# A hybrid layer's state-space scan on Trainium2: rotated second products against transfers that swap real and imaginary rows

## The reference

```python
xn = rmsnorm(x, norm_g)
u_a, z_a, q, k, v, z_b, g_a, g_b = split(xn @ w_in)
# S5: 64 groups of 16 channels, 64 complex states each
h[t] = a_bar * h[t-1] + b_bar @ u[t]            # complex
y_a = real(C @ h) + D * u                       # also returned: h at the last position
y_a = gelu(y_a); y_a = y_a * sigmoid(y_a @ glu_w + glu_b) * silu(z_a)
o = stick_breaking_attention(q, k, v) * silu(z_b)
x + (sigmoid(g_a) * (y_a @ w_a) + sigmoid(g_b) * (o @ w_b)) @ w_out, then rmsnorm
```

## Time and profile before

| | |
|---|---|
| median of 3 runs | 3242.06 us (3238.5 to 3243.9) |
| the profiled execution | 3239.77 us, span 3238.0 us |
| TensorE busy | 3127.3 us (97%), 20272 products |
| VectorE, ScalarE, GpSimd busy | 1007.5, 999.5, 756.1 us |
| mean granted TensorE clock | 0.985 of full speed |
| 160 loads of w_in | 512 KB each, 3.9 us to landing |

### The profile page before, as it was taken

The page is one execution under the profiler, slowest core; times in us unless marked ns, Lnnn a source line. Parts: engine busy times, 40 slices in busy tenths (PEclk is TensorE's granted clock), DMA queues, the critical chain, the costliest instruction groups (busy, mean ns, idle before and its releaser), DMA issues.

```text
span 3238.0 us, 50469 instructions
## 1 busy us (share of the span) xinstructions
PE 3127.3 (97%) x20272; PEld 3047.1 (94%) x20272; DVE 1007.5 (31%) x1345; ACT 999.5 (31%) x1258; POOL 756.1 (23%) x2309
## 2 busy tenths in 40 slices
PE   7999999999999999999999999999999999999997
PEld 6998999999899999989999998999899999999997
DVE  5124212312421231242123124212465214332265
ACT  5225214422531442253144225214421101121142
POOL 5620550163055016305501630550013000000000
PEclk9999999999999999999999999999999989999999
DMA  5221122222112222211222221122339545342283
GB/s 170 58 83 59 52 78 71 69 59 83 59 52 78 68 73 59 83 59 52 78 68 73 59 83 59 52 78 69 128 124 293 176 150 177 98 137 71 65 246 106
DMA packets 395785, 304.10 MB, mean 94 GB/s; under 512 B 57314, under 2 KB 364082, under 8 KB 393522
## 3 DMA queue, kind: packets, MB, share of 16 engines
q1 hardware_dynamic: 395570, 301.05, 30.4%
HBM read 227.30 MB, written 65.27 MB: 90 GB/s over the span
## 4 chain that ended last, share of the span: by engine, by line
PE 84%; POOL 5%; ACT 3%; DVE 3%; issue 2%; DMA 1%; SPq 1%; POOLq 0%; DVEq 0%; ACTq 0%
PE acc L1652 71%; PE side L1613 5%; PE side L1821 2%; PE side L1876 1%; PE side L1816 1%; PE acc L1613 1%; ACT L809 1%; POOL work L1164 1%; POOL work L1161 1%; DMA t_oz<-work 1%; POOL work L1158 1%; DMA work<-t_state_seeds 1%; POOL work L1165 1%; POOL work L1160 1%; DVE work L1419 1%
## 5 line engine op out<-in xcount | busy, mean ns | idle before, releaser
L1652 PE MATMUL acc<-x_high,w_high 128*128 128x344 f32 (+2 forms) x5440 | 1230.1, 329 | 15.3 <-issue 3.8
L1652 PE MATMUL acc<-x_low,w_high 128*128 128x344 f32 (+2 forms) x5440 | 1186.3, 321 | 0.0
L1652 PE MATMUL acc<-x_high,w_low 128*128 128x344 f32 (+2 forms) x5440 | 1180.7, 320 | 0.0
L1652 PEld LDWEIGHTS acc<-x_high,w_high 128*128 128x128 f32 x5440 | 913.5, 190 | 41.1 <-issue 23.3
L1652 PEld LDWEIGHTS acc<-x_low,w_high 128*128 128x128 f32 x5440 | 927.2, 190 | 0.0
L1652 PEld LDWEIGHTS acc<-x_high,w_low 128*128 128x128 f32 x5440 | 917.0, 189 | 0.0
L1277 DVE TENSOR_TENSOR w_low<-w_raw,w_high 128x1024 fp32r<-128x1024 f32 x233 | 298.9, 1283 | 1038.2 <-ACT w_high L815 1037.9
L815 ACT CAST w_high<-w_raw 128x1024 fp32r<-128x1024 f32 x232 | 242.9, 1047 | 992.4 <-PE acc L1652 931.3
L1148 POOL COPY work<-s_tables 128x28 f32 x16 | 3.3, 207 | 1370.1 <-DMA work<-t_state_seeds 1370.1
L1613 PE MATMUL side<-work 128*128 128x128 f32 (+6 forms) x832 | 152.7, 308 | 9.7 <-DVE work L1405 9.7
L1613 PEld LDWEIGHTS side<-work 128*128 128x128 f32 (+3 forms) x832 | 100.2, 159 | 43.0 <-issue 25.6
(11 more groups left out here) (296 smaller groups left out, 2524.9 us busy)
## 6 DMA issues: line engine op xcount, KB each, us to landing
w_raw<-in_w_in SPq DMA_DIRECT2D x160, 512.0 KB, 3.9
w_raw<-in_w_out SPq DMA_DIRECT2D x48, 512.0 KB, 4.0
work<-t_sig_ga SPq DMA_DIRECT2D x24, 516.0 KB, 4.5
out<-work SPq DMA_DIRECT2D x18, 512.0 KB
t_sig_gb<-stage SPq DMA_DIRECT2D x16, 516.0 KB, 4.2
t_qk<-stage SPq DMA_DIRECT2D x16, 516.0 KB, 5.2
work<-t_qk SPq DMA_DIRECT2D x16, 516.0 KB, 4.1
t_sig_ga<-stage SPq DMA_DIRECT2D x16, 516.0 KB, 4.1
```

Of the source, the lines that this page charges most:

```text
L1652: ins = mm(acc[s][:, a, 0:n], w[b][:, kk, :], x[:, kx, c0:c0 + n], start=start, stop=stop)
```

## The change

M2 is still computed but no longer transposed, and the products with B2T are gone. VectorE copies the first products from `side` to T2, and two transfers put T2's real rows into the imaginary rows of `swapped_p` and the reverse; this takes the place of Q. After the scan the same is done with T2 into `swapped_t`, and V1 alone holds the rotated states; V2, its products with N2 and its last-state product are gone. The imaginary half of the table `ei` is negated once, in the prologue. VectorE's work is split over PQ, SCAN and ROT. The steps BT, KM, PQ, YM, YS and YT move. Some `one` become `tr`. Semaphores are renamed or dropped (`seed_mm` becomes `par_mm`).

```diff
-DVE_A = 24
+DVE_A = 26
-    B2T = c.take(512).rearrange("p (g s) -> p g s", g=HG)
+    swapped_p = c.take(512)
-    V2 = v_flat[:, 516:1032].rearrange("p (g j) -> p g j", g=HG)
+    swapped_t = v_flat[:, 516:1028]
...
+            def swap(ready, count, dst, src):
+                sp.wait_ge(ready, count)
+                sp.dma_start(dst[0:64], src[64:128]).then_inc(swap_in, 16)
+                sp.dma_start(dst[64:128], src[0:64]).then_inc(swap_in, 16)
...
                 if cn == 4:
                     toeplitz(0)
+                    swap(p_copied, i * 2 + 1, swapped_p, T2)
+                if cn == 5:
+                    swap(t_ready, i * 2 + 1, swapped_t, T2)
                 if cn == 6:
                     s5_states(0)
                     s5_params(1)
+                if cn == 8:
+                    toeplitz(1)
+                if cn == 9:
+                    swap(p_copied, i * 2 + 2, swapped_p, T2)
+                    swap(t_ready, i * 2 + 2, swapped_t, T2)
                 if cn == 10:
-                    toeplitz(1)
+                    s5_states(1)
+                if cn == 11:
+                    s5_out()
                 if cn == 12:
-                    s5_states(1)
-                    s5_out()
                     attn_load()
...
-    BT, KM, PQ, YM, YS = (9, 33), (13, 35), (15, 37), (18, 41), (19, 42)
-    XJ, UG, US, YT = 10, 11, 12, 43
+    BT, KM, PQ, SCAN, ROT, YM, YS = (9, 27), (13, 30), (15, 33), (17, 35), (19, 37), (21, 39), (22, 40)
+    XJ, UG, US, YT = 10, 11, 12, 41
...
-                        nc.scalar.copy(B2T, side[:, 1, :].rearrange("p (g s) -> p g s", g=HG)).then_inc(bt_ready, 1)
...
-                        nc.scalar.copy(fs, side[0:HG, 1, 0:2 * P]).then_inc(fin_copied, 1)
+                        act.wait_ge(st_sent, i * 128 + 64 * hf + PRIMED)
+                        nc.scalar.copy(fo, side[0:HG, 1, 0:P]).then_inc(fin_ready, 1)
...
+        step(G.tensor_scalar(ei[64:128], ei[64:128], -1.0, None, ALU.mult))
...
+                        V.tensor_copy(T2, side[:, 0, :]).then_inc(p_copied, 1)
                         ch(V.tensor_tensor(T1, side[:, 0, :], e_r, ALU.mult))
-                        ch(V.tensor_tensor(T2, side[:, 1, :], e_i, ALU.mult))
-                        ch(V.tensor_tensor(T1, T1, T2, ALU.add))
+                    if p == SCAN[hf]:
+                        dve.wait_ge(swap_in, i * 128 + (64 * hf + 32))
+                        ch(V.tensor_tensor(swapped_p, swapped_p, Ei.rearrange("p g j -> p (g j)"), ALU.mult))
+                        ch(V.tensor_tensor(T1, T1, swapped_p, ALU.add))
                         for g in range(HG):
                             last_op = V.tensor_tensor_scan(T2[:, g * NCH:(g + 1) * NCH],
...
-                        ch(last_op)
-                        V.memset(V2[:, :, 0:1], 0.0)
-                        V.tensor_tensor(V2[:, :, 1:NCH + 1], Ei, T2g, ALU.mult).then_inc(v_ready, 1)
+                        last_op.then_inc(t_ready, 1)
+                        dve.wait_ge(t_ready, 2 * i + hf + 1)
+                        ch(V.tensor_tensor(V1[:, :, 1:NCH + 1], Er, T2.rearrange("p (g j) -> p g j", g=HG), ALU.mult))
+                    if p == ROT[hf]:
+                        dve.wait_ge(swap_in, i * 128 + (64 * hf + 64))
+                        ch(V.tensor_tensor(tsg, tsg, Ei, ALU.mult))
+                        V.tensor_tensor(V1[:, :, 1:NCH + 1], V1[:, :, 1:NCH + 1], tsg, ALU.subtract).then_inc(v_ready, 1)
                     if p == YM[hf]:
-                        V.tensor_tensor(fo[:, 0:64], fs[:, 0:64], fs[:, 192:256], ALU.subtract)
-                        V.tensor_tensor(fo[:, 64:128], fs[:, 64:128], fs[:, 128:192], ALU.add).then_inc(fin_ready, 1)
...
-                            last_op = tr(side[:, 1, g * P:(g + 1) * P], M2[:, g, :], ident[:, :])
...
-                            last_op = one(side[:, 1, g * P:(g + 1) * P], B2T[:, g, :], Ug[:, HG * hf + g, :])
...
-                            mm(out, V2[:, g, 0:NCH], N2[:, g, GC:9 * GC], start=False, stop=True)
-                        one(side[0:HG, 1, 0:P], V1[:, :, NCH], ident[:, :])
-                        one(side[0:HG, 1, P:2 * P], V2[:, :, NCH], ident[:, :])
+                        tr(side[0:HG, 1, 0:P], V1[:, :, NCH], ident[:, :])
...
-                            last_op = one(side[0:NEW, 0, g * P:(g + 1) * P], hn[:, g, :], ident[:, :])
+                            last_op = tr(side[0:NEW, 0, g * P:(g + 1) * P], hn[:, g, :], ident[:, :])
...
-                        last_op = one(side[0:NEW, 0, n * P:(n + 1) * P], src[:, SEQ:TOK], ident[:, :])
+                        last_op = tr(side[0:NEW, 0, n * P:(n + 1) * P], src[:, SEQ:TOK], ident[:, :])
```

More of the change, by code:

```diff
@@ L208, in build @@
     ysT = c.take(P, NEW)
-    fs = c.take(2 * P, HG)
     fo = c.take(P, HG)
@@ L274, in build @@
     u_ready = sem("u_ready")
-    s5_in, seed_in, seed_mm, seed_ready, s_seed_ready, seed_out, m_ready, n_ready, e_ready, ha_ready = [sem(s) for s in
-        ("s5_in", "seed_in", "seed_mm", "seed_ready", "state_seed_ready", "seed_out", "s5_m_ready", "s5_n_ready", "s5_e_ready", "s5_ha_ready")]
+    s5_in, seed_in, seed_ready, s_seed_ready, seed_out, m_ready, n_ready, e_ready, ha_ready = [sem(s) for s in
+        ("s5_in", "seed_in", "seed_ready", "state_seed_ready", "seed_out", "s5_m_ready", "s5_n_ready", "s5_e_ready", "s5_ha_ready")]
     b_mm, bt_ready, k_mm, kt_ready, kt_pad, toep_in = [sem(s) for s in
         ("s5_b_mm", "s5_bt_ready", "s5_k_mm", "s5_kt_ready", "s5_kt_pad", "s5_toep_in")]
-    xj_mm, xj_ready, ug_mm, ug_ready, pq_mm, v_ready, y_mm, yj_ready, fin_copied, fin_ready = [sem(s) for s in
+    xj_mm, xj_ready, ug_mm, ug_ready, pq_mm, v_ready, y_mm, yj_ready, fin_ready, p_copied, t_ready, swap_in = [sem(s) for s in
         ("s5_xj_mm", "s5_xj_ready", "s5_ug_mm", "s5_ug_ready", "s5_pq_mm", "s5_v_ready", "s5_y_mm",
-         "s5_yj_ready", "s5_fin_copied", "s5_fin_ready")]
+         "s5_yj_ready", "s5_fin_ready", "s5_p_copied", "s5_scanned", "s5_swapped_in")]
     hn_ready, ys_mm, ys_ready, yt_mm, yt_ready, y_sent, st_sent = [sem(s) for s in
@@ L779, in _ @@
             x_high(n)
-        act.wait_ge(seed_mm, 1)
+        act.wait_ge(par_mm, 2)
         nc.scalar.mul(C_neg.rearrange("p (a n) -> p a n", a=2), side[:, :, :], -1.0).then_inc(seed_ready, 1)
@@ L838, in phase_a @@
                         act.wait_ge(b_mm, 2 * i + hf + 1)
-                        nc.scalar.copy(B1T, side[:, 0, :].rearrange("p (g s) -> p g s", g=HG))
-                        nc.scalar.copy(B2T, side[:, 1, :].rearrange("p (g s) -> p g s", g=HG)).then_inc(bt_ready, 1)
+                        nc.scalar.copy(B1T, side[:, 0, :].rearrange("p (g s) -> p g s", g=HG)).then_inc(bt_ready, 1)
                     if p == KM[hf]:
@@ L1333, in _ @@
             x_low(n)
-        dve.wait_ge(seed_mm, 2)
+        dve.wait_ge(par_mm, 3)
         V.tensor_scalar(S_neg[0:64].rearrange("p (g b) -> p g b", b=NEW), acc[0][0:64, 0, :].rearrange("p (b g) -> p g b", b=NEW), -1.0, None, ALU.mult)
@@ L1365, in phase_a @@
                         dve.wait_ge(toep_in, (i * 2 + (hf + 1)) * (16 * CH))
-                        e_r, e_i = [e.rearrange("p g j -> p (g j)") for e in (Er, Ei)]
+                        e_r = Er.rearrange("p g j -> p (g j)")
+                        V.tensor_copy(T2, side[:, 0, :]).then_inc(p_copied, 1)
                         ch(V.tensor_tensor(T1, side[:, 0, :], e_r, ALU.mult))
-                        ch(V.tensor_tensor(T2, side[:, 1, :], e_i, ALU.mult))
-                        ch(V.tensor_tensor(T1, T1, T2, ALU.add))
+                    if p == SCAN[hf]:
+                        dve.wait_ge(swap_in, i * 128 + (64 * hf + 32))
+                        ch(V.tensor_tensor(swapped_p, swapped_p, Ei.rearrange("p g j -> p (g j)"), ALU.mult))
+                        ch(V.tensor_tensor(T1, T1, swapped_p, ALU.add))
                         for g in range(HG):
@@ L1665, in first_tile @@
                 last = tr(side_flat[:, k * P:(k + 1) * P], C_rows[:, k, :], ident[:, :])
-            last.then_inc(seed_mm, 1)
+            last.then_inc(par_mm, 1)
             for k in range(4):
                 last = tr(acc[0][:, 0, k * P:(k + 1) * P], S_rows[:, k, :], ident[:, :])
-            last.then_inc(seed_mm, 1)
+            last.then_inc(par_mm, 1)
             for n in range(KT + 3, KT + 6):
@@ L1723, in phase_a @@
                         for g in range(HG):
-                            tr(side[:, 0, g * P:(g + 1) * P], M1[:, g, :], ident[:, :])
-                            last_op = tr(side[:, 1, g * P:(g + 1) * P], M2[:, g, :], ident[:, :])
+                            last_op = tr(side[:, 0, g * P:(g + 1) * P], M1[:, g, :], ident[:, :])
                         last_op.then_inc(b_mm, 1)
@@ L1740, in phase_a @@
                         for g in range(HG):
-                            one(side[:, 0, g * P:(g + 1) * P], B1T[:, g, :], Ug[:, HG * hf + g, :])
```

(8 more changed lines are left out.)

9 lines of the change are left out of this document (2 added, 7 removed).

## The result

The changed kernel takes **3294.6 us** (median of 4 runs, 3291.1 to 3298.0) against 3243.0 for the kernel before: ratio 1.0166, 95% interval 1.0153 to 1.0178. It is slower by 51.6 us. The forecast was 3315 in a range of 3294 to 3345; the sign and the mechanism held, and the size lies 0.6 us inside the low edge of the range. That is less than the spread of the runs, so that it fell inside is luck. The profiled execution took 3293.3 us, its span is 3291.5 us, 53.5 more than before.

The account below looks back on a forecast made before the run. TensorE, busy 97% of the span, was taken to bound the kernel. Over eight passes, 106 us of standing still plus 19 of clock less 52 of saved instructions gave +73: 3242 + 73 = 3315 us, range 3294 to 3345.

Parts of the forecast that it names:

- the mechanism: At second-half BT[1], TensorE stands still waiting for GpSimd's M, whose start hangs on YM[0], YS[0] and SP's parameters.
- The sum: Per pass: p = 39 moves by +11.2 us, slots behind it save 2.07, so +9.1 us, +73 in eight.
- The stop: At BT[1], TensorE asks for M at 999.7, M is ready at 1012.9: 13.2 us a pass, 106 in all.
- YS: State products becoming transposes, eight instructions to four, save 0.44 us a half.
- The clock: After the stop at BT[1], TensorE's clock runs at half, losing 2.4 us a pass, ends 1.7 and 3.4.
- Behind YM[1]: After YM[1], shorter slots save 1.3 + 0.44 + 0.33 = 2.07 us a pass.
- BT[0]: At p = 9, TensorE's present wait of 1.45 us for GpSimd's tables was expected to remain.
- The swaps: Two 128 KB transfers, twice a half, 3.0 us each time (ends 2.0 and 3.8); cost to TensorE 0 in both halves.
- the second rival: Slow swaps: 3.8 us transfers queued behind the weight load stop TensorE at YM[0]; about +3 us a pass, 3340; chance 0.2.
- BT's place hardly matters: Were BT[1] not late, VectorE's chain alone would stop TensorE from 1036.2 to 1051.4 at YM[1].

Follow-up runs that it names:

- the shorter tables: The changed kernel with GpSimd leaving out the last M2 and N2 columns, which nothing reads any more; 3276.0 us.
- the earlier parameters: The changed kernel with SP fetching the second half's parameters after YS[0], before storing the first half's states; 3285.4 us.
- without the swaps: The changed kernel with VectorE not waiting for swaps and using T2's own rows; SP sends small transfers to an unused place; 3294.0 us.
- The late steps: The changed kernel with second-half steps later: BT 32, KM 34, PQ 37, SCAN 40, ROT 42, YM 44, YS 45, YT 46; 3224.0 us.
- the combined run: The changed kernel with late steps (BT 31 to YT 45), shorter tables, parameters before stores and YS as products; 3188.4 us.
- BT of the second half later: The changed kernel with second-half BT moved from 27 to 32, KM 30 to 33, PQ 33 to 34; 3326.9 us.

## Why the prediction was right, and where its sizes were off

**The mechanism held.** GpSimd's second start was forecast 54.3 us after BT[0] and came at 54.7; the stop stood where forecast, at the M1 transposes of the second half; YM[0] and YM[1] had no wait; the instruction count was exact. The runs with the shorter tables, the earlier parameters and without the swaps show it by three separate changes. The late steps and the combined run show that the saved instructions are worth about their time once the stop is gone.

**The sum was 9.1 us a pass and is 6.8 in the mean, 6.9 in the fourth pass.** Term by term, in the fourth pass:

- *The stop: 13.2 forecast, 12.0 measured.* Three errors: GpSimd started 0.4 us later and TensorE arrived 0.6 us later than forecast (next point), and M was 1.05 us shorter. I left one collision with VectorE's split inside M (18.95 us). M took 17.9, as with none. The step that failed is that the split of p = 28 falls before M. ScalarE rounds that chunk, and in its program the copy of BT[1] stands ahead; it waited 21.06 us for the transposes, and the split waited behind it (23.71 us, above). The timeline of ScalarE:

```profile
1033.76 0.59 ACT L852 COPY work<-side 128x512 f32<-128x512 f32 x1 [21.06 <-PE side L1737]
1034.24 1.05 ACT L828 CAST w_high<-w_raw 128x1024 fp32r<-128x1024 f32 x1
```

  I had asked who queues behind TensorE's wait on TensorE, but wrote of ScalarE that it waits for nothing new. The Trainium skill (SBUF — State Buffer, who interferes with whom) has a VectorE instruction with two inputs from SBUF shut out a GpSimd one that reads SBUF. The trace agrees: the split began at 1035.32, outside M, and M was shorter than forecast by about one blocked instruction. (The second of the two blocked before was of another shape than I wrote, 1.38 us where its like take 0.40; the sum changes by under 0.1 us.)
- *YS: 0.44 us saved forecast, nothing saved.* From YS[0] to the arrival at BT[1] it took 15.6 us, not 15.04: 0.44 are these, the rest is that the wait counts from the end of the last big product and I had counted starts. I priced a transpose between small products by a row of eight transposes in a line. The error comes again in YS[1], inside the term behind YM[1].
- *The clock: 2.4 forecast, 3.0 measured* (half of 6.0; 2.5 in the mean of the passes), inside its ends. YM[1] came 39.3 us after BT[1], not 38.9.
- *Behind YM[1]: 179.4 forecast, 178.0 measured.* The half clock behind the stop of 3.12 us is there in all eight passes before (a mean granted clock of 0.72 to 0.77 over the 6 us behind it). In the changed kernel it is there in the first, second and eighth (0.72) and not in the others (1.00), this one among them. Where it stays away a pass gains 1.4 to 1.7 us. I had carried it over as fixed. Why it stays away is open.
- *BT[0]: 0.2 to 0.5 us of waiting in place of 0.8 to 1.5*, in these two passes. The parameters of the first half landed about 1 us sooner after their issue. Why was not tried.

Together 0.6 (the later arrival) - 1.2 + 0.4 - 1.5 - 0.5 = -2.2, and 9.1 - 2.2 = 6.9.

**The swaps** were sized at 3.0 us to landing and took 2.3:

```profile
work<-work SPq DMA_DIRECT2D x64, 128.0 KB, 2.3
```

So VectorE's chain is 10.8 us, not 12.2, and the second rival had no ground. The Trainium skill (DMA: Bandwidth & Descriptors, anatomy of one DMA) fits 2.0 us and the bytes over 436 GB/s to transfers that GpSimd issues. By that fit, an estimate here since SP issues these, a swap takes 2.3 us, and the trace agrees with it better than with the row to DRAM that I took.

The order of VectorE's program was misread in one place: the split of p = 36 stands ahead of the rotation at p = 37, not behind it (it began at 1067.34, the rotation's product with the swapped rows at 1069.39). It ran while VectorE would have waited for the swap, so it cost nothing.

**One sentence was too strong.** I wrote that BT's place hardly matters because VectorE's chain stops TensorE anyway. The stop does move, but the kernel then took 32 us more. Most of that is the clock: its mean over the span was 0.966 in place of 0.974, about 27 us.

## What to carry to other kernels

Before steps are moved in a hand-written order, find the longest chain on the other engines that starts at one moved step and ends at another, and compare its length with the steps between them: here GpSimd's 45 us began behind YM[0] and was needed by YM[1], and the change cut the distance from 23 steps to 18. A saving of instructions on the engine that bounds is real only once that chain fits; the same swaps gave 3327, 3324, 3295 and 3224 us by the places of the steps alone, and 3188 with the chain made shorter. A queue with a fixed order ties unrelated waits together, so look for what is queued behind every engine that will wait.

## What the runs showed of the hardware

The loss behind a stop of TensorE is not set by the stop's length. In one run (BT of the second half later) a stop of 9.84 us was followed by a mean granted clock of 0.77 over 9.7 us of work, and one of 9.85 us, a pass later, by 0.50, the 1.2 GHz level throughout. A stop of 12.0 us in the change was followed by 6.0 us at that level, one of 10.75 us in the run with the parameters first by 4.4, and the stop of 3.12 us by 3 us or so in eight passes of eight before and by none in five of eight after.

A transpose 128 columns wide between small float32 products makes a group start every 0.34 us where the two-instruction product makes 0.27, although transposes in a row cost 0.11 each and such products 0.22. The slot of four groups up to the next big product took 1.19 and 1.17 us, so neither form was the cheaper.

A VectorE split of 1.23 to 1.5 us that ran into GpSimd's table work held up one GpSimd instruction: 1.35 us in place of 0.29 before, and 1.71 in place of 0.73 in the change (at 1035.72).
